# Quarter-size head sums, pairwise squares and an earlier start of layer two's weights in a two-layer float32 block

## What is computed

```python
def rms_norm(x, g):
    y = xf * lax.rsqrt(jnp.mean(xf * xf, axis=-1, keepdims=True) + EPS)
...
q = rms_norm(q.reshape(B, S, N_HEADS, HEAD_DIM), g_q[l]) * (HEAD_DIM ** -0.5)
k = rms_norm(k.reshape(B, S, N_HEADS, HEAD_DIM), g_k[l])
...
x = x + mix @ w_out[l]
h = rms_norm(x, g_ffn[l])
x = x + (jax.nn.silu(h @ w_gate[l]) * (h @ w_up[l])) @ w_down[l]
...
h = rms_norm_2(x, norm_g) * (1 + scale[:, None]) + shift[:, None]
proj = h @ w_in
xa, za, q, k, v, zb, qi, ki, wi, ga, gb = jnp.split(proj, IN_SPLITS, axis=-1)
```

## Time and profile before

| | |
|---|---|
| median of 3 runs | 1014.56 us (1014.4 to 1015.97) |
| profiled execution | 1014.74 us, span 1013.2 us |
| TensorE matmul busy | 992.9 us, 98% of the span |
| VectorE busy | 678.0 us, 67% |
| ScalarE busy | 436.4 us, 43% |
| GpSimd busy | 156.8 us, 15% |
| mean granted TensorE clock | 0.996 of full speed |

### The profile page before, as it was taken

How to read it: one execution, slowest core, us unless ns; L and a number is a source line. 1 busy time by engine, 2 the same in 40 slices (tenths; PEclk the granted TensorE clock), 3 DMA queues, 4 the chain that set the end, 5 groups by cost and what they waited for, 6 DMA issues and landing times.

```text
span 1013.2 us, 14459 instructions
## 1 busy us (share of the span) xinstructions
PE 992.9 (98%) x4724; PEld 806.1 (80%) x4724; DVE 678.0 (67%) x1207; ACT 436.4 (43%) x721; POOL 156.8 (15%) x270
## 2 busy tenths in 40 slices
PE   7999999999999999999999999999999999999996
PEld 6787787777888888888888886888888887777886
DVE  6787786796766756645526568398987765665755
ACT  5546666543432323323311235845552325563333
POOL 3000100100000000865000000745660000000000
PEclk9999999999999999999999999999999999999999
DMA  7254624252443333344222222322233332112322
GB/s 228 64 159 132 195 75 144 66 148 79 135 134 93 94 102 92 96 145 134 97 104 87 99 74 83 105 84 83 63 102 86 104 99 67 42 62 84 103 84 84
DMA packets 145168, 104.11 MB, mean 103 GB/s; under 512 B 4636, under 2 KB 136988, under 8 KB 145132
## 3 DMA queue, kind: packets, MB, share of 16 engines
q1 hardware_dynamic: 139792, 85.96, 28.1%
q0 software_dynamic: 5104, 17.64, 5.6%
q10 hardware_dynamic: 236, 0.06, 0.0%
HBM read 99.45 MB, written 4.19 MB: 102 GB/s over the span
## 4 chain that ended last, share of the span: by engine, by line
PE 93%; DVE 3%; ACT 2%; issue 1%; DMA 1%; SPq 0%; DVEq 0%; ACTq 0%
PE bank L570 19%; PE bank L572 19%; PE bank L571 19%; PE bank L804 4%; PE bank L803 4%; PE bank L805 4%; PE bank L548 2%; PE bank L555 2%; PE bank L636 2%; PE bank L556 2%; PE bank L557 2%; PE bank L719 1%; PE bank L721 1%; PE bank L720 1%; PE bank L610 1%
## 5 line engine op out<-in xcount | busy, mean ns | idle before, releaser
L570 PE MATMUL bank<-hH,wH 128*128 128x512 f32 x848 | 333.1, 393 | 0.8 <-DVE wL L1446 0.5
L572 PE MATMUL bank<-hH,wL 128*128 128x512 f32 x848 | 330.1, 389 | 0.0
L571 PE MATMUL bank<-hL,wH 128*128 128x512 f32 x848 | 330.0, 389 | 0.0
L1029 ACT ACTIVATE wH<-raw 128x1024 fp32r<-128x1024 f32 x156 | 165.3, 1060 | 276.6 <-PE bank L572 136.3
L1446 DVE TENSOR_TENSOR wL<-raw,wH 128x1024 fp32r<-128x1024 f32 x156 | 197.2, 1265 | 128.3 <-ACT wH L1029 127.5
L570 PEld LDWEIGHTS bank<-hH,wH 128*128 128x128 f32 x848 | 159.2, 188 | 36.3 <-issue 2.2
L571 PEld LDWEIGHTS bank<-hL,wH 128*128 128x128 f32 x848 | 159.2, 188 | 33.5 <-issue 1.0
L572 PEld LDWEIGHTS bank<-hH,wL 128*128 128x128 f32 x848 | 159.2, 188 | 33.1
L805 PE MATMUL bank<-aH,wL 128*128 (+1 forms) x176 | 68.5, 389 | 0.0
L803 PE MATMUL bank<-aH,wH 128*128 (+1 forms) x176 | 68.5, 389 | 0.0
L804 PE MATMUL bank<-aL,wH 128*128 (+1 forms) x176 | 68.5, 389 | 0.0
(11 more groups left out here) (449 smaller groups left out, 1483.2 us busy)
## 6 DMA issues: line engine op xcount, KB each, us to landing
raw<-in_w_in_dram SPq DMA_DIRECT2D x61, 512.0 KB, 3.5
mraw<-in_w_mod_dram POOLq DMA_DIRECT2D x24, 512.0 KB, 4.5
raw<-in_w_gate_dram SPq DMA_DIRECT2D x22, 512.0 KB, 3.6
raw<-in_w_up_dram SPq DMA_DIRECT2D x22, 512.0 KB, 3.6
raw<-in_w_down_dram SPq DMA_DIRECT2D x22, 512.0 KB, 3.2
raw<-in_w_out_dram SPq DMA_DIRECT2D x16, 512.0 KB, 3.6
x_tok<-in_x_dram SPq DMA_DIRECT2D x4, 512.0 KB, 5.9
rotations<-eb POOLq DMA_DIRECT2D x4, 512.0 KB, 5.0
```

The costliest lines, as they stand in the source:

```text
L570: mm(o, a, hH[:, k, :], start=(k == 0), stop=False)
L571: mm(o, a, hL[:, k, :], start=False, stop=False)
L572: ins = mm(o, b, hH[:, k, :], start=False, stop=(k == KD - 1))
L1029: return A(o, i_, ACT.Copy, scale=scale)
```

## The change

Four things, in the order of the program:

- `head_sums`: each of the two full sums becomes two of 64 rows by 64 columns, with `ones` in place of `bdones`. The sum of the queries takes rows and columns of the same half, that of the keys crosses halves; so that it comes out in the right place, ScalarE writes the squares of the keys with halves exchanged, in two instructions.
- Squares 0 and 1 of layer one's output are still summed alone, behind blocks 3 and 4. Of squares 2 to 7, VectorE adds each pair (`pair_add`), behind blocks 4, 6 and 7, and TensorE sums the pair behind blocks 5 and 7 and in the first feed-forward projections. ScalarE's next square waits for the sum or the addition that reads its buffer.
- `w_transposes(1)` stands ahead of `keys_two`, each group behind the copy that frees its bank.
- The first projection of `xa` has halves of its own, `wxH` and `wxL`. ScalarE makes `wxH` behind the fifth block of `hH`, VectorE makes `wxL` behind the last block of `hL`.

```diff
+        wxH, wxL = at("wxH", [P, 1024], F32R, A0 + 32768), at("wxL", [P, 1024], F32R, A0 + 36864)
...
-            def project(s, m=P, each=None):
+            def project(s, m=P, each=None, halves=None):
...
+                hi, lo = halves or (wH[s.par], wL[s.par])
                 for k in range(KD):
-                    a, b = wH[s.par][:, k * P:k * P + m], wL[s.par][:, k * P:k * P + m]
+                    a, b = hi[:, k * P:k * P + m], lo[:, k * P:k * P + m]
...
-                for e, sq in enumerate((sqq, sqk)):
-                    mm(SB[e][:], bdones, sq[:], start=True, stop=True).then_inc(ss_mm, 1)
+                settled(pe)
+                lo, hi = slice(0, HD), slice(HD, P)
+                for e, sq, rows in ((0, sqq, (lo, hi)), (1, sqk, (hi, lo))):
+                    for r, c in zip(rows, (lo, hi)):
+                        ins = mm(SB[e][c, :], ones[r, c], sq[r, :], start=True, stop=True, skip_group_check=True)
+                    ins.then_inc(ss_mm, 1)
...
-                mm(PB[4][:], ones[:], (sqx, a32)[d % 2][:], start=(d == 0), stop=(d == KD - 1), skip_group_check=True
-                   ).then_inc(ss_used if d < KD - 1 else ssm, 1)
-            due = {3: (0,), 4: (1, 2), 5: (3,), 6: (4,), 7: (5,)}
+                mm(PB[4][:], ones[:], (sqx, a32)[d][:], start=(d == 0), stop=False, skip_group_check=True
+                   ).then_inc(ss_used, 1)
+
+            def pair_sum(j):
+
+                pe.wait_ge(sq_pair, j)
+                mm(PB[4][:], ones[:], a32[:], start=False, stop=(j == 3), skip_group_check=True
+                   ).then_inc(ss_used if j < 3 else ssm, 1)
             for d in range(3, KD):
...
-                for k in due[d]:
-                    square_sum(k)
-
-            def square_sums():
-                square_sum(KD - 2)
-                square_sum(KD - 1)
-            project_two(N_FF, x1l, 1, 2, square_sums)
+                if d < 5:
+                    square_sum(d - 3)
+                elif d % 2:
+                    pair_sum(d // 2 - 1)
+            project_two(N_FF, x1l, 1, 2, lambda: pair_sum(3))
...
                 for b in range(4):
-                    wait(pe, wt_ev, 4 * half)
+                    if half:
+                        pe.wait_ge(wt_ev, b + 1)
...
+            w_transposes(1)
             keys_two()
-            w_transposes(1)
-            project(Slot(N_XA))
+            project(Slot(N_XA), halves=(wxH, wxL))
...
-                    A(sq[:], PB[sl.par][:], ACT.Square).then_inc(gfree[sl.par], 1)
+                    if sq is sqq:
+                        A(sq[:], PB[sl.par][:], ACT.Square).then_inc(gfree[sl.par], 1)
+                    else:
+                        A(sq[HD:P, :], PB[sl.par][0:HD, :], ACT.Square)
+                        A(sq[0:HD, :], PB[sl.par][HD:P, :], ACT.Square).then_inc(gfree[sl.par], 1)
...
-                if d > 1:
-                    act.wait_ge(ss_used, d - 1)
+                if d == 2:
+                    act.wait_ge(ss_used, 1)
+                elif d > 2 and d % 2:
+                    act.wait_ge(ss_used, d // 2 + 1)
+                elif d > 2:
+                    act.wait_ge(sq_pair, d // 2 - 1)
                 A((sqx, a32)[d % 2][:], xT[:, d, :], ACT.Square).then_inc(xsq_rdy, 1)
...
+            xa = Slot(N_XA)
             for d in range(KD):
                 act.wait_ge(h2f, d + 1)
                 A(hH[:, d, :], (sg, a32)[d % 2][:], ACT.Identity, bias=mod[:, d:d + 1]).then_inc(h2h, 1)
+                if d == 4:
+                    act.wait_ge(w_full[0], xa.half * 16 + 16)
+                    act.wait_ge(slot_used, N_DN + KF)
+                    copy(wxH[:], raw[0][:]).then_inc(hi_done, 1)
             kv, ki = Slot(N_KV, 0), Slot(N_KV, 1)
             used(kv)
-            split_hi(kv.next())
...
+            def pair_add(d):
+                dve.wait_ge(xsq_rdy, d + 1)
+                TT(a32[:], a32[:], sqx[:], AD).then_inc(sq_pair, 1)
+
             for d in range(KD):
...
                 TT(xT[:, d, :], xT[:, d, :], wo2[d % 2][:], AD).then_inc(x1_rdy, 1)
+                if d > 2 and d % 2 == 0:
+                    pair_add(d - 1)
                 if 0 < d < KD - 1:
                     split_lo(Slot(N_WO, d + 1).next())
             x1_low(KD - 1)
+            pair_add(KD - 1)
...
-            split_lo(Slot(N_KV, 0).next())
+            dve.wait_ge(hi_done, N_XA + 1)
+            TT(wxL[:], raw[0][:], wxH[:].bitcast(F32), SU).then_inc(lo_done, 1)
```

More of the change, by code:

```diff
@@ L273, in program @@
         tr_mm, t_free, pv, o_free, yo_rdy = (sem(n) for n in ("tr_mm", "t_free", "pv", "o_free", "yo_rdy"))
-        ssum, ssm, rr, rc_mean, xsq_rdy, ss_used = (sem(n) for n in ("ssum", "ssm", "rr", "rc_mean", "xsq_rdy", "ss_used"))
+        ssum, ssm, rr, rc_mean, xsq_rdy, ss_used, sq_pair = (
+            sem(n) for n in ("ssum", "ssm", "rr", "rc_mean", "xsq_rdy", "ss_used", "sq_pair"))
         x1_rdy, x1h, x1l = sem("x1_rdy"), sem("x1h"), sem("x1l")
```

## The result

The changed kernel takes 1008.99 us, the median of five runs (1008.95 to 1009.15). Against the kernel before on the same chip the ratio is 0.9938, 95% interval 0.9928 to 0.9949; one execution of the kernel before that took 3546 us is not in it. Forecast were 1007.1 us within 1005.9 to 1010.8.

The account below looks back on a forecast made before the run. TensorE, busy 98% of the span, was taken as the bound. Savings of 2.4 (head sums), 1.5 (squares), 1.8 (weights) and 1.8 (clock) sum to 7.5 us: 1014.74 to 1007.24, less 0.18 is 1007.1 us; range 1005.9 to 1010.8.

Parts of the forecast that it names:

- Head sums, 2.4 forecast: Four groups of head sums: four quarters run side by side, 0.86 us a group instead of 1.72; 2.4 us saved.
- The rival at 1013.9: Head sums: quarters with different rows block each other in one PSUM bank, 4.4 us lost; chance 0.07.
- two quarters at a time (1010.5): Head sums: only two quarters run side by side, so 2.4 us saved becomes -1.0; chance 0.10.
- one after another (1017.4): Head sums: quarters run in sequence, 3.44 us a group, 2.4 us saved becomes -7.9; chance 0.06.
- Squares, 1.5 forecast: Squares of layer one's output: eight sums become five, 2.6 us less, partly given back in waits; 1.5 us net.
- The wait behind block 7: Layer one's output: TensorE newly waits 1.1 us for VectorE's pair addition before the sum.
- The 0.2 behind block 5: Layer one's output: TensorE newly waits 0.2 us for VectorE's pair addition before the sum.
- the wait for the last `hL` that falls away: After layer one's squares: TensorE comes later and no longer waits for the last `hL` block; 0.3 us back.
- Weights, 1.8 forecast: Start of layer two: second transposes fill idle ahead of the keys, 2.05 us gone, 0.24 wait added; net 1.8 us.
- The clock, 1.8 forecast: Layer-two keys: with the idle filled, the granted clock stays full and the keys end 1.8 us earlier.
- The rival that transposes don't keep the clock (1008.9): Layer-two keys: the clock falls despite the filled gap, so its 1.8 us don't come; chance 0.12.
- two rivals: Range's upper part: two quarters side by side, 1010.5, chance 0.10; lead lost at a later wait, 1010.4, chance 0.04.

Follow-up runs that it names:

- the last experiment: Changed kernel plus 12 warm-up transposes, third pair's square sum behind the first four feed-forward blocks, first pair's `wL` ahead of the keys' low halves: 1007.64 us, ratio 0.9928.
- head sums alone: Kernel before with only the head sums in quarters and the keys' squares crossed: 1013.24 us, ratio 0.9981.
- squares alone: Kernel before with only the squares of layer one's output added in pairs: 1013.10 us, ratio 0.9982.
- halves alone: Kernel before with own weight halves for the first `xa` projection, second weight transposes left behind the keys: 1014.29 us, ratio 0.9991.
- the kernel before with the filled start: Kernel before with 12 more warm-up transposes of the first tokens on TensorE, 4 ahead of and 8 behind the vectors' transpose: 1014.55 us, ratio 1.0001.
- the changed kernel's second profile: Changed kernel run again with no edit: 1009.15 us, ratio 0.9934 against the kernel before.

## Why the prediction was right, and where not

It forecast 7.5 us less than the profiled execution before; that execution and the one after differ by 7.1 on the ruler, and by 5.8 in all. Point by point:

- **Head sums, 2.4 forecast, 2.2 to 2.3 found.** The group is where it was put: four quarters side by side. It takes 0.7 less in the loop where 0.66 was counted, and 0.67 - 0.09 = 0.58 less ahead of it where 0.46 was counted, since the changes of shape cost up to 0.1 less than the earlier trace rows suggested. On the ruler, which leaves the 0.09 out, that makes 2.8. But the first pair gives 0.6 back: from its head sums to the next it is 43.25 us and was 43.32. The step that failed is that each group's gain was carried to the end without a look at who is late next in that pair. The projections behind the group come 0.7 us earlier, and the third of them waits for VectorE's `wL`; behind that, VectorE's maxima of the first head hold the scores, so that even without the wait 0.2 of the 0.67 stay lost (42.84 us, the last experiment). The timelines of ScalarE and VectorE in the changed kernel have the reason; the chain starts from ScalarE's two table loads (1.28 us each), the first of which starts ahead of the end of the head sums' group, and in VectorE's queue the halves of the keys stand ahead of `wL`:

```profile
38.86 1.28 ACT L1188 ACT_TABLE_LOAD   x1
```

```profile
48.97 0.69 DVE L1653 TENSOR_TENSOR k1L<-kn,k 64x512 fp32r<-64x512 f32 x1
49.68 1.22 DVE L1469 TENSOR_TENSOR wL<-raw,wH 128x1024 fp32r<-128x1024 f32 x1
```

  Counted from the first head sums, that `wL` starts at 49.68 - 38.06 = 11.62 us, and before at 48.50 - 36.81 = 11.69: the chain got next to nothing of the gain.

- **The bank.** The Trainium skill (TensorEngine Tiling (Array Packing), Gotcha 1: PSUM Pressure) says that different row tiles can't use one PSUM bank at the same time. Here both quarters of `sqq` have different rows and one bank, and start together (165.78); the trace does not agree, at least for quarters that write different partitions of the bank. The rival at 1013.9 is refuted, and so are those with two quarters at a time (1010.5) and one after another (1017.4): uncrossed quarters, which are two at a time, cost 0.85 us more per group.
- **Squares, 1.5 forecast, 1.7 found.** The wait behind block 7 is as forecast: 0.91 us of idle, 242.00 - 240.93 = 1.07 from the end of the block (its last record starts at 240.70, and 0.23) to the sum. The 0.2 behind block 5 came too, though no idle shows it, since a record is longer than the distance to the next start: 229.07 - (228.66 + 0.23) = 0.18. The term mis-sized is the wait for the last `hL` that falls away. It was taken at its idle, 0.28, and entered as 0.3; by starts it was 250.85 - (250.19 + 0.23) = 0.43, and the matmul behind it 0.1 slower. With that and a slower start behind each of the two new waits it is 2.6 - 1.07 - 0.18 - 0.2 + 0.53 = 1.7. TensorE in the changed kernel, then in the kernel before:

```profile
228.66 0.39 PE L728 MATMUL bank<-mixH,wL 128*128 128x512 f32 x1
229.07 1.12 PE L779 MATMUL bank<-a,ones 128*128 128x512 f32 x2
...
240.70 0.39 PE L728 MATMUL bank<-mixH,wL 128*128 128x512 f32 x1
```

```profile
250.19 0.39 PE L586 MATMUL bank<-hH,wL 128*128 128x512 f32 x1
```

- **Weights, 1.8 forecast, 1.9 to 2.0 found.** The transposes fit ahead of `hL`, and the own projection starts 0.16 us behind the keys, where 0.24 was counted for bank 0.
- **The clock, 1.8 forecast, 1.3 found, and it is not a constant.** The step that failed first: the keys were taken to end, at full clock, one block of 1.4 us behind VectorE's last `hL`. The timeline of VectorE in the changed kernel shows the last two low halves close together:

```profile
623.02 0.75 DVE L1968 SCALAR_TENSOR_TENSOR hL<-sg,mod,hH 128x512 fp32r<-128x512 f32 x1
623.90 0.75 DVE L1968 SCALAR_TENSOR_TENSOR hL<-a,mod,hH 128x512 fp32r<-128x512 f32 x1
```

The one before last ends at 623.77; TensorE starts that block at 623.87 and has two blocks of 1.4 us to do, not one: 626.7. The last wait that binds was the seventh half's, not the eighth's. In the kernel before the seventh ends at 625.71 + 0.75 = 626.46; two blocks behind it would be 629.4 by the same distances, an estimate, and 630.66 - 629.4 = 1.3. The second step that failed: one profile was taken as the rule. The low clock behind the idle came in the profile before, and not in four other executions with the same idle (head sums alone, squares alone, halves alone, the kernel before with the filled start). Against the median it is worth only its share of the executions. The rival that transposes don't keep the clock (1008.9) is not supported: the clock was 1.00 through the keys in all seven profiles with the filled gap, but as it also was in four of five with the gap open, that alone would prove little. The start shows it better (below).
- **The start** stood in no term: 1.25 us of difference between two executions, 0.80 of it later tokens, 0.35 the clock and 0.1 the change of shape ahead of the first head sums. With it the sum closes: 7.1 - 1.25 = 5.8.

So the forecast time of 1007.1 was 1.9 us too low, within its range, with the mechanisms as described; it was low because the profile before was an execution with an early start (36.81 us, where the other eleven profiles have 37.26 to 39.40) and a fall at the keys, and both were read as the kernel. That the range held all the same is in part luck: its upper part was set to reach two rivals, and no term of it stood for the start or for a fall that comes only in some executions.

## What to carry to other kernels

When a wait is filled with moved work, look what the work covered where it stood: the transposes paid only because the next projection got halves of its own. When TensorE's work shrinks ahead of a chain on VectorE, ask for the first place where that chain is tied to something that did not get earlier; here it took a fifth of the head sums' gain. And split a gain that hangs on the clock from the rest, since one profile shows one outcome of several.

## What the runs showed of the hardware

- Four float32 matmuls of 64 rows and 64 columns on the four quarters of the array, two with different rows in each of two banks, run side by side: a group of four takes 1.02 us to the next matmul's start, two whole ones 1.83. Two on the same quarters follow each other.
- An idle of 1.9 us on TensorE is followed by a granted clock of 0.50 in one profile and of 1.00 in four others, of kernels with the same instructions there; the runs of one kernel in two groups say that it differs between executions of one program too. At the keys one fall cost 1.3 us, at the start about 0.3 or, where it lasted about twice as long, 1.6 (26.86 - 25.30).
- At the start of the changed kernel the clock came back from 0.50 to 1.00 between 15.5 and 15.7 us, while TensorE had done nothing but transposes since 12.41 and did so until 17.57 (the windows 14.00:15.50 and 15.70:17.50 above). The Trainium skill (TensorE: Matmul & The Clock Gate, Part 4: PE-mode transpose) says that transposes don't count as a busy TensorE in the same way; here the trace shows the clock rise behind float32 transposes alone (whether they use the mode that the page speaks of, it does not show). It took about 3.1 us of them here and about 6 us in the changed kernel's second profile, from 12.54 to 18.5 (0.53 from 16.00 to 18.70), still among transposes.
